# Up stage of a streaming-encoder block: VectorE's order between the adds, one-hots read from PSUM, more early sparse rows, GpSimd's low weights in four column pieces

## What is computed

```python
hn = rms_norm(h, norm2_gain)
qry = (hn @ w_query).reshape(tokens, 8, 2, 128)
s1 = einsum('thd,hnd->thn', qry[:, :, 0], sub_keys1)      # 128 keys each
s2 = einsum('thd,hnd->thn', qry[:, :, 1], sub_keys2)
v1, i1 = top_k(s1, 16);  v2, i2 = top_k(s2, 16)
cand = v1[..., :, None] + v2[..., None, :]                 # 256 pairs
top_s, pos = top_k(cand, 16);  idx = (i1 * 128 + i2)[pos]
gate = softmax(top_s)
pre = einsum('td,thkd->thk', hn, expert_down[idx])
act = gelu(pre) * gate
h = h + einsum('thk,thkd->td', act, expert_up[idx])        # 8 heads x 16 experts a token
```

## Time and profile before

| | us |
|---|---|
| median of 3 runs | 4082.46 (4072.62 to 4082.53) |
| profiled execution | 4070.29 |
| its span | 4068.5 |
| TensorE busy | 3875.3 (95%), granted clock 0.976 |
| VectorE busy | 2516.9 (62%) |
| GpSimd busy | 1974.0 (49%) |
| ScalarE busy | 1329.1 (33%) |

### The profile page before, as it was taken

How to read it: one execution, slowest core, us unless ns; L and a number is a source line. 1 busy time by engine, 2 the same in 40 slices (tenths; PEclk the granted TensorE clock), 3 DMA queues, 4 the chain that set the end, 5 groups by cost and what they waited for, 6 DMA issues and landing times.

```text
span 4068.5 us, 51118 instructions
## 1 busy us (share of the span) xinstructions
PE 3875.3 (95%) x20037; PEld 3481.8 (86%) x20037; DVE 2516.9 (62%) x4060; ACT 1329.1 (33%) x1587; POOL 1974.0 (49%) x631
## 2 busy tenths in 40 slices
PE   7999999999999999998999999998899999999999
PEld 6667677776688878998999999998899999989999
DVE  5444555555575235898788888854556656666664
ACT  5333334444322222322344434432222222222222
POOL 2232232232344433565565665675555565565564
PEclk9999999999999999999999999999899999999999
DMA  3322222222234222466677787798777777777773
GB/s 145 114 95 78 82 77 78 78 80 80 96 134 183 108 101 93 167 245 233 249 294 280 298 303 277 300 357 343 269 264 254 265 267 250 269 264 253 264 262 124
DMA packets 175542, 811.04 MB, mean 199 GB/s; under 512 B 13568, under 2 KB 71168, under 8 KB 92544
## 3 DMA queue, kind: packets, MB, share of 16 engines
q1 hardware_dynamic: 59232, 399.47, 26.8%
q0 software_dynamic: 36864, 268.45, 18.2%
q10 hardware_dynamic: 79264, 140.56, 9.7%
HBM read 741.32 MB, written 72.35 MB: 200 GB/s over the span
## 4 chain that ended last, share of the span: by engine, by line
PE 80%; DVE 12%; ACT 2%; DVEq 2%; issue 2%; DMA 2%; POOL 0%; ACTq 0%; SPq 0%
PE ps L1259 73%; PE ps L1478 2%; DVE psm L871 2%; PE ps L1341 2%; DMA g_exp<-g_dram 1%; DVEq L1116 1%; DVE expert_rows L1108 1%; DVE scores L875 1%; PE ps L1324 1%; PE ps L1333 1%; DVE s_all L1097 1%; DVE s_all L1099 1%; PE ps L1275 0%; DVE h_dense L1211 0%; ACT w_hi L340 0%
## 5 line engine op out<-in xcount | busy, mean ns | idle before, releaser
L301 POOL TENSOR_TENSOR w_e_lo<-w_e_raw,w_e_hi 128x2048 fp32r<-128x2048 f32 x256 | 1183.8, 4625 | 559.3 <-ACT w_e_hi L621 557.4
L294 POOL TENSOR_TENSOR w_lo<-w_raw,w_hi 128x2048 fp32r<-128x2048 f32 x115 | 541.2, 4706 | 1080.9 <-ACT w_hi L340 1080.9
L1259 PE MATMUL ps<-act_hi,w_e_hi 128*128 128x384 f32 x2048 | 713.3, 348 | 114.6 <-DVE act_lo L1192 87.4
L1259 PE MATMUL ps<-sn_hi,w_e_hi 128*128 128x384 f32 x2048 | 695.1, 339 | 12.8 <-POOL w_e_lo L301 12.8
L1259 PE MATMUL ps<-act_lo,w_e_hi 128*128 128x384 f32 x2048 | 706.9, 345 | 0.0
L1259 PE MATMUL ps<-act_hi,w_e_lo 128*128 128x384 f32 x2048 | 706.1, 345 | 0.0
L621 ACT ACTIVATE w_e_hi<-w_e_raw 128x2048 fp32r<-128x2048 f32 x256 | 489.9, 1914 | 634.4 <-PE ps L1259 257.4
L1259 PE MATMUL ps<-sn_lo,w_e_hi 128*128 128x384 f32 x2048 | 686.5, 335 | 0.0
L1259 PE MATMUL ps<-sn_hi,w_e_lo 128*128 128x384 f32 x2048 | 686.4, 335 | 0.0
L1211 DVE TENSOR_TENSOR h_dense<-ps,h_dense 128x384 f32<-128x384 f32 x512 | 279.1, 555 | 484.8 <-PE ps L1259 477.7
L1259 PEld LDWEIGHTS ps<-act_hi,w_e_hi 128*128 128x128 f32 x2048 | 402.3, 196 | 125.0 <-DVE act_lo L1192 97.3
(11 more groups left out here) (224 smaller groups left out, 5254.0 us busy)
## 6 DMA issues: line engine op xcount, KB each, us to landing
w_e_raw<-w_stream SPq DMA_DIRECT2D x256, 1024.0 KB
w_raw<-w_stream SPq DMA_DIRECT2D x116, 1024.0 KB, 4.8
gel_dram<-gel_all ACTq DMA_DIRECT2D x32, 768.0 KB
g_dram<-gate_buf ACTq DMA_DIRECT2D x12, 2048.0 KB, 7.4
gel_in<-gel_dram ACTq DMA_DIRECT2D x32, 768.0 KB
g_exp<-g_dram ACTq DMA_DIRECT2D x32, 768.0 KB
gate_dram<-g_raw ACTq DMA_DIRECT2D x32, 256.0 KB, 2.0
g_in<-gate_dram ACTq DMA_DIRECT2D x16, 512.0 KB, 5.9
```

The lines of the kernel that those rows point to most:

```text
L294: nc.gpsimd.tensor_tensor(wlo[s][:, :], raw[s][:, :], whi[s][:, :].bitcast(F32), ALU.subtract).then_inc(lo_ready, 1)
L301: nc.gpsimd.tensor_tensor(e_lo[j % 4][:, :], e_raw[j % 4][:, :], e_hi[j % 3][:, :].bitcast(F32), ALU.subtract).then_inc(lo_ready, 1)
L1259: m = mm(ps[:, bank, 0:width], lhs[:, w], r, start=(n % (3 * per) == 0), stop=(n % (3 * per) == 3 * per - 1))
```

## The change

1. GpSimd's `low` forms the low weights of an expert tile in four instructions of 512 columns instead of one of 2048.
2. In the up stage VectorE's products and low halves stand singly between the adds; the last low half of a group comes behind add 12. ScalarE makes the four high halves as two and two, behind the weight copies of the group's first two tiles. A tile's row add comes behind its third quarter.
3. The one-hots read the line 0..127 from PSUM bank 3 (`key_line`); oh2 loses its multiplication by one. The gates then have bank 2 alone, so TensorE waits for ScalarE's copy of the gate before (`g_sb`, n instead of n - 1).
4. 36 instead of 20 down rows are dotted before the gates: `top_of_heads` is cut in two (`pick_of_heads`), with four dots before each half. T_EXP, T_TURN and T_GATES move seven tiles back, `used_by` has nine entries, gates and dots run up to tiles 112 and 113.
5. T_ACT moves from tile 122 to 114. Ten up rows are added early, one per tile from 115 to 124 instead of two per tile. The first group's load is issued at tile 116 instead of 124, its products are formed at 119, high halves at 120 and low halves at 121, instead of all at the end of the stage.
6. The sparse sum is turned one tile earlier, and its adds follow their group.

```diff
@@ -44,15 +44,16 @@
-T_EXP = 29
-T_TURN = 31
-T_GATES = 34
-GATE_TILE = [T_GATES + 4 * n // 5 for n in range(N_GATES)]
-FIRST_ROWS = 20
-DOT_TILE = [T_GATES + 8 * j // 9 for j in range(85)] + [110 + j // 2 for j in range(PAIRS - FIRST_ROWS - 85)]
+T_EXP = 36
+T_TURN = 38
+T_GATES = 41
+GATE_TILE = [T_GATES + 3 * n // 4 for n in range(N_GATES)]
+FIRST_ROWS = 36
+DOT_TILE = [T_GATES + 4 * j // 5 for j in range(PAIRS - FIRST_ROWS)]
 T_ACT = DOT_TILE[-1] + 1
-ADD_TILE = [T_ACT + 1 + j // 2 for j in range(10)] + [EXPERT_TILES + 1 + j for j in range(PAIRS - 10)]
-T_SPARSE_OUT = EXPERT_TILES + 122
+ADD_TILE = list(range(T_ACT + 1, EXPERT_TILES - 3))
+ADD_TILE += [EXPERT_TILES + 1 + j for j in range(PAIRS - len(ADD_TILE))]
+T_SPARSE_OUT = ADD_TILE[-1] + 3
...
@@ -298,8 +299,11 @@
                 pool.wait_ge(hi_ready, b + 1)
-                nc.gpsimd.tensor_tensor(e_lo[j % 4][:, :], e_raw[j % 4][:, :], e_hi[j % 3][:, :].bitcast(F32),
-                                        ALU.subtract).then_inc(lo_ready, 1)
+                for q in range(4):
+                    part = slice(512 * q, 512 * q + 512)
+                    e = nc.gpsimd.tensor_tensor(e_lo[j % 4][:, part], e_raw[j % 4][:, part],
+                                                e_hi[j % 3][:, part].bitcast(F32), ALU.subtract)
+                e.then_inc(lo_ready, 1)
...
@@ -316,7 +320,7 @@
             issued = 0
-            used_by = [8, 13, 18, 22, 26]
+            used_by = [9, 12, 15, 18, 21, 25, 28, 31, 34]
...
@@ -658,7 +662,7 @@
                 act.wait_ge(g_mm, n + 1)
-                nc.scalar.activation(quad(g_first[:, :]) if q == 0 else in_group(q), quad(ps[:, GB + n % 2, :]),
+                nc.scalar.activation(quad(g_first[:, :]) if q == 0 else in_group(q), quad(ps[:, GB, :]),
...
@@ -696,21 +700,21 @@
                     nc.scalar.activation(gt[:, :], ps[:, GB, 0:TD], ACT.Copy).then_inc(gthi_ready, 1)
+                if t == T_ACT:
+                    act.wait_ge(pre3_ready, 1)
+                    nc.scalar.activation(act3[:, :], act3[:, :], ACT.Gelu).then_inc(gelu3_ready, 1)
...
                 down(t)
-                if t == T_ACT:
-                    act.wait_ge(pre3_ready, 1)
-                    nc.scalar.activation(act3[:, :], act3[:, :], ACT.Gelu).then_inc(gelu3_ready, 1)
...
                     load_group(0, 0)
-                if t == EXPERT_TILES - 2:
+                if t == T_ACT + 6:
...
@@ -731,8 +735,8 @@
                             peer_hi(EXPERT_TILES + 4 * g + q + 2)
-                        if q == 0 and g + 1 < GROUPS:
-                            for e in range(4):
+                        if q < 2 and g + 1 < GROUPS:
+                            for e in (2 * q, 2 * q + 1):
...
@@ -1083,6 +1087,10 @@
                 v.drain()
+
+            def pick_of_heads(blk, four):
+
+                first = 16 * KEYS * blk + 8 * KEYS * four
...
@@ -1121,21 +1129,27 @@
             sparse = slice(P * SPARSE, P * SPARSE + P)
-            top_of_heads(SPARSE, 0)
-            top_of_heads(0, 0)
+            for blk in (SPARSE, 0):
+                top_of_heads(blk, 0)
+                pick_of_heads(blk, 0)
...
             top_of_heads(SPARSE, 1)
+            pick_of_heads(SPARSE, 1)
...
             top_of_heads(1, 0)
+            pick_of_heads(1, 0)
...
             for k, (blk, four) in enumerate(((2, 0), (0, 1), (1, 1), (2, 1))):
-                for j in range(SLOTS * k, SLOTS * k + SLOTS):
+                for j in range(2 * SLOTS * k, 2 * SLOTS * k + SLOTS):
...
                 top_of_heads(blk, four)
+                for j in range(2 * SLOTS * k + SLOTS, 2 * SLOTS * (k + 1)):
+                    dot(j)
+                pick_of_heads(blk, four)
...
@@ -1155,6 +1169,9 @@
             v.drain()
+            key_line = ps[:, GB + 1, 0:KEYS]
+            vec.tensor_copy(key_line, iota[:, :])
+            v.drain()
...
@@ -1162,9 +1179,8 @@
                     tok = slice(4 * n + t, 4 * n + t + 1)
-                    vec.tensor_scalar(oh2[r][:, KEYS * t:KEYS * (t + 1)], iota[:, :], i2_t[:, tok], ones[:, 0:1],
-                                      ALU.is_equal, ALU.mult)
-                    e = vec.tensor_scalar(g_oh[r][:, KEYS * t:KEYS * (t + 1)], iota[:, :], i1_t[:, tok], gt[:, tok],
+                    vec.tensor_scalar(oh2[r][:, KEYS * t:KEYS * (t + 1)], key_line, i2_t[:, tok], None, ALU.is_equal)
+                    e = vec.tensor_scalar(g_oh[r][:, KEYS * t:KEYS * (t + 1)], key_line, i1_t[:, tok], gt[:, tok],
...
@@ -1195,10 +1211,11 @@
                     add_row(j)
-                if ADD_TILE[j] == EXPERT_TILES - 1 and ADD_TILE[j + 1] > EXPERT_TILES:
+                if ADD_TILE[j] == T_ACT + 5:
...
                         product(0, e)
+                if ADD_TILE[j] == T_ACT + 7:
...
@@ -1210,28 +1227,61 @@
+            def add_rows_of(t):
+                for j in range(PAIRS):
+                    if ADD_TILE[j] == t:
+                        add_row(j)
+
+            def add_sparse():
+
+                v.wait_ge(h3_in, 16)
+                for k in range(4):
+                    v.wait_ge(acc3_tr, k + 1)
+                    part = h_sparse[:, 512 * k:512 * (k + 1)]
+                    vec.tensor_tensor(part, ps[:, ROWS + k, :], part, ALU.add).then_inc(h3_done, 1)
+
             for g in range(GROUPS):
-                s, more = 1 - g % 2, g + 1 < GROUPS
-                for q in range(4):
-                    if q == 1 and more:
-                        v.wait_ge(up_in[s], 32 * ((g + 1) // 2) + 32)
-                        for e in range(4):
-                            product(s, e)
-                    for f in range(4 * q, 4 * q + 4):
-                        add_dense(g, f)
-                    if q >= 2 and more:
-                        for e in (2 * q - 4, 2 * q - 3):
-                            low(4 * g + 4 + e, s, e)
-                    t = EXPERT_TILES + 4 * g + q
-                    for j in range(PAIRS):
-                        if ADD_TILE[j] == t:
-                            add_row(j)
-                    if t == T_SPARSE_OUT + 1:
-                        v.wait_ge(h3_in, 16)
-                        for k in range(4):
-                            v.wait_ge(acc3_tr, k + 1)
-                            part = h_sparse[:, 512 * k:512 * (k + 1)]
-                            vec.tensor_tensor(part, ps[:, ROWS + k, :], part, ALU.add).then_inc(h3_done, 1)
+                s, n, t = 1 - g % 2, 4 * g + 4, EXPERT_TILES + 4 * g
+                more = g + 1 < GROUPS
+                add_dense(g, 0)
+                if more:
+                    v.wait_ge(up_in[s], 32 * ((g + 1) // 2) + 32)
+                    product(s, 0)
+                add_dense(g, 1)
+                if more:
+                    product(s, 1)
+                add_dense(g, 2)
+                add_rows_of(t)
+                add_dense(g, 3)
+                if more:
+                    product(s, 2)
+                add_dense(g, 4)
+                if more:
+                    product(s, 3)
+                add_dense(g, 5)
+                if more:
+                    low(n, s, 0)
+                add_dense(g, 6)
+                add_rows_of(t + 1)
+                add_dense(g, 7)
+                add_dense(g, 8)
+                if more:
+                    low(n + 1, s, 1)
+                add_dense(g, 9)
+                if more:
+                    low(n + 2, s, 2)
+                add_dense(g, 10)
+                add_rows_of(t + 2)
+                add_dense(g, 11)
+                add_dense(g, 12)
+                if more:
+                    low(n + 3, s, 3)
+                add_dense(g, 13)
+                add_dense(g, 14)
+                add_rows_of(t + 3)
+                add_dense(g, 15)
+                if t <= T_SPARSE_OUT < t + 4:
+                    add_sparse()
...
@@ -1473,14 +1523,14 @@
                 pe.wait_ge(oh_ready, n + 1)
-                need(pe, g_sb, n - 1)
+                need(pe, g_sb, n)
                 for t in range(4):
-                    m = mm(ps[:, GB + r, KEYS * t:KEYS * (t + 1)], oh2[r][:, KEYS * t:KEYS * (t + 1)],
+                    m = mm(ps[:, GB, KEYS * t:KEYS * (t + 1)], oh2[r][:, KEYS * t:KEYS * (t + 1)],
...
             for t in range(EXPERT_TILES):
-                extras = {24 + 12 * k: [lambda n=n: gates(n)]
+                extras = {12 + 24 * k: [lambda n=n: gates(n)]
```

## The result

The kernel after took 4128.9 us (median of 4 runs, 4121.0 to 4138.2) where the kernel before took 4078.8 (4072.6 to 4082.5): a ratio of 1.0133, interval 1.0117 to 1.0148. It is slower by 1.3%; the prediction of 3905 was wrong in sign. The profiled execution took 4122.7 us.

What follows compares the result with a forecast made beforehand. TensorE was taken to bound the kernel, so only its idle and slow time could go. Down stage 2803.7, first group 53.4, 31 x 33.3 = 1032.3 and tail 2.9 gave span 3892, forecast 3905 us, range 3880 to 3975.

Steps and rivals of the forecast that it cites:

- The pieces: GpSimd's w_e_lo: three more instructions per tile at 0.1 us each, hidden, with VectorE assumed to get in between.
- the wait of at most 1.2 us: Up stage: longest wait of a VectorE two-SBUF instruction on w_e_lo, if a piece's end lets it in.
- the earlier gather: Up stage: row add behind the third quarter, so gather and w_e_lo start about 2 us earlier.
- the 14.27 us row of L1152: Profile row cited against a way in: VectorE was shut out at both borders of three w_e_lo in a row.
- The first rival's walk: Up stage: pieces give no way in; three 4.2 us waits make 33.5 a group, a fourth 37.7; 3973 us, chance 0.20.
- The third rival: Up stage: pieces costing 0.95 us more under the same lock, 41.9 us a group, 4171 us; chance 0.10.
- The low halves in front of the last quarter: Up stage: last low half behind add 12 removes TensorE's stops of 3.03 and 1.48 us, giving 33.3 us a group.
- the new top-k order: Down stage's top-k part: half blocks with four dots remove TensorE's two stops, 16 us won (bounds 0 and 16).
- The first group: Start of the up stage: 53.4 us instead of 66.0, gain 12.6 (bounds 5 and 20), with one stop of about 20.
- The one-hots from PSUM: Down stage with gates: 0.4 us each, 186 us of VectorE's time saved, winning nothing by itself.

Runs made afterwards that it cites:

- e9: Kernel after with one edit, each gather of an up row asked for one tile later: 3889.6 us, 0.9546.
- e2: Kernel before with the column pieces of the low weights alone: 4102.5 us, 1.0073.
- e4: Kernel after with each column piece waiting by a semaphore for the end of the piece before: 3889.9 us, 0.9552.
- e5: Kernel after with w_e_lo as one whole instruction and each gather of an up row one tile later: 3895.5 us, 0.9573.
- e1: Kernel after with w_e_lo again as one instruction of 2048 columns: 4086.2 us, 1.0031.
- e3: Kernel after with whole w_e_lo and the up stage's order of before: 4039.5 us, 0.9914.
- e6: Kernel after with whole w_e_lo, later gathers, and VectorE's two-SBUF instructions in pairs at tile borders: 3902.9 us, 0.9572.
- e12: Kernel after with whole w_e_lo, later gathers, and one-hots reading the line from SBUF again: 3894.5 us, 0.9559.
- e10: Kernel before with each gather of an up row asked for one tile later, nothing else: 3980.9 us, 0.9779.

## Why the prediction was wrong, by its own steps

**The pieces, and the ring: the step that failed.** Two terms failed together: the wait of at most 1.2 us, which was 4.8 to 5.3, and the earlier gather, which I had put at no cost and which brought each w_e_lo right behind it. GpSimd's wait for the row add was there before, but had slack; four waits of 5 us a group used it up. I wrote "If VectorE gets in at a piece's end, a wait is at most 1.2 us", named the 14.27 us row of L1152 against it and still made the way in my forecast. The row was right: that w_e_lo, at 1910.85, had also followed a gather, at 0.02 us:

```profile
1909.89 0.94 POOL L309 DMA_INDIRECT expert_rows<-down_rows,idx  x1 [1.27 <-DVE expert_rows L1108]
```

By the Trainium skill (SBUF — State Buffer, "SBUF: two separate sides") whoever starts first gets the port pair for the whole instruction, and the other is blocked. The trace agrees in that VectorE's two-SBUF instructions wait for the end of a GpSimd piece; it differs in who was first, as the low half of 3169.58 is recorded 0.41 us before w_e_lo and waited all the same. Whether the waiting side is next the page does not say, and here it is not, unless GpSimd had to wait before the first piece (e9, and e2's down stage) or between the pieces (e4).

**The first rival's walk was mis-sized.** It had 20.9 + 3 x 4.2 = 33.5 us, with a fourth wait 37.7; measured was 41.65, about 20.9 + 4 x 5.1. Three terms were off. (a) "By a margin of 0.4 us none behind row 2": a low half that begins 0.41 us before w_e_lo (3169.58 and 3169.99) is already shut out; all four rows have their wait. (b) A wait is 4.8 to 5.3 us (the 5.39 to 5.85 us of an instruction less its own 0.55), not 4.2. (c) The walk took w_e_lo's start after the row add as given and asked only whether VectorE's sum fits into 33.3. But that start is what makes the waits full length each time. e5 cuts this with one number, leaves the lock whole and comes to 33.3; e9 does it for the kernel after. So the lock alone did not make the change slower, nor the ring alone: either e4 (open the lock) or e9 (cut the ring) turns 4129 into 3890.

I had "a row's add comes behind the third quarter, so GpSimd's gather, and w_e_lo behind it, start about 2 us earlier" and put it at no cost or a gain. In the kernel before, w_e_lo was held back by ScalarE's copies about once a group, at the very place where the four products stood, and so they ran with no wait:

```profile
2977.95 1.96 DVE L1187 TENSOR_TENSOR gel_in<-gel_in,g_exp 128x384 f32<-128x384 f32 x4
```
```profile
2982.36 4.63 POOL L301 TENSOR_TENSOR w_e_lo<-w_e_raw,w_e_hi 128x2048 fp32r<-128x2048 f32 x1 [3.03 <-ACT w_e_hi L621]
```

The new order brought each w_e_lo right behind its gather. This was the sentence to follow up: which instruction will stand in front of it then?

**The third rival** had the right sign and place but the wrong price. It wanted 0.95 us a piece; a piece costs (5.03 - 4.60) / 3 = 0.14, and I had taken 0.1. Its 41.9 us a group came close by luck: three waits of 7.0 where there were four of about 5.1.

**What held.** The low halves in front of the last quarter do free TensorE: with the ring cut a group is 33.3 us (e9: 3887.7 us of span where I had 3892). The down stage ended at 2801 (2803.7), but I had credited the whole gain to the new top-k order. (Its term was 5.27 + 7.55 + 2 x 1.5 = 15.8, entered as 16.4; nothing hangs on the difference.) Pieces alone, in the old order, give it too (e2: 2803.0), and the new order with whole w_e_lo keeps one stop of 6.7 to 6.8 us in e1, e3 and e6. The first group took 54.9 us (53.4), by another path: TensorE stopped for 3.67 us, for an add that waited for the load of h_dense, and 9.31 for a product, not once for about 20, and then the ring's first waits came. The idle steps in the top-k part are gone in the kernel after. The one-hots from PSUM take 0.343 and 0.402 us (I took 0.4), never longer than 0.406, where the maximum was 4.7, and win nothing by themselves (e12).

```profile
L1182 DVE TENSOR_SCALAR oh<-ps,i_t x384: 337/343/352, 1980.4 to 2657.5; 128x128 f32<-128x128 f32 x192
```

**What stays open.** Why VectorE is let in after a wait of GpSimd's and not behind a gather: that GpSimd's next instructions are already queued in the second case fits all rows, but no run shows the queue. Why e1, e3 and e6, with whole w_e_lo, have a stop of nearly 7 us in the top-k part and e5 and e12 have not. Their runs point at executions, not kernels: those of e1 lie at 4081 to 4082 and at 4090 to 4092, of e3 at 4034 and 4045, of e6 at 3894 and 3902 to 3904, of e5 at 3895 and 3904, and each of the three traces with the stop is of the upper cluster, e5's without it of the lower. But only one execution of each was traced, the kernel after has two clusters as well (4121 to 4123, 4135 to 4138) and no stop in its trace, which is of the lower, and the trace of the kernel before, also of its lower cluster, has both stops. So this is not shown.

## What to carry to other kernels

Where two engines share something exclusively, don't ask only how long one holds it; follow the order around: if A's next turn waits, through a third step, for B to get through, the waits never shrink. One slack slot in that ring, here a gather asked for a tile later, made the reordering pay: the new order alone stood at 4086 us (e1), the later gather alone at 3981 (e10, which lacks the down stage's 32 us), the two together at 3896 (e5). Splitting an instruction helped the one who waits only where the splitter had stopped, between the parts or just before the first. And when an edit makes a step start earlier "for free", look at what it will then stand in front of.

## What the runs showed of the hardware

- A GpSimd tensor_tensor (two inputs, float32) of 2048, 1024 and 512 columns took 4.61, about 2.54 (two in 5.08) and 1.29 us; a piece that follows at once starts 1.25 us after the one before.
- A VectorE TENSOR_TENSOR with two SBUF inputs whose start is recorded 0.41 us before that of a GpSimd tensor_tensor right behind a gather waited for its end (3169.58 and 3169.99). One that starts 0.86 us before is done by then (3158.57 and 3159.44). The adds, with one input in PSUM, never took more than 0.56 us in the up stage.
- How long TensorE stood still did not decide alone what its granted clock did next. In the kernel after it was 0.50 behind a stop of 3.46 us (from 3144.40, at 335 GB/s beside it) and behind one of 1.87 (from 3052), but 1.00 behind one of 3.47 (from 3227.60). After the 1.58 us stops of e10 it stayed at 1.00 over the whole stretch, which spares the 1.5 us of slow steps in a group.

```profile
3144.40:3147.40 3.00, 3.00 (x10) 3.00 (x11) 2.91 (x3) 1.72 (x1) 0.00 (x0) 0.50 0.92 335
3052.00:3055.30 3.30, 3.30 (x12) 3.30 (x11) 3.30 (x4) 0.00 (x0) 0.80 (x1) 0.50 0.00 0
3227.60:3231.00 3.40, 3.36 (x19) 3.36 (x20) 3.31 (x4) 1.92 (x1) 0.00 (x0) 1.00 0.86 309
```
```profile
2880.00:3860.00 980.00, 935.67 (x5354) 926.73 (x5353) 612.84 (x781) 264.68 (x224) 623.64 (x223) 1.00 0.79 284
```
